# A four-layer decoder trunk: the second product of its MLPs by seven half-size products for eight

## The chip, the cores and the metric

The kernel runs on one NeuronCore of a Trainium2 chip. A core has a matrix engine (TensorE, PE in the profile, its weight loads PEld), three engines for elementwise work (VectorE, DVE; ScalarE, ACT; GpSimd, POOL) and SyncE (SP), which here only issues DMAs. The metric is the device time of one execution in microseconds (us); before the change it is 2807.53 us, the median of three runs (2807.37 to 2809.55).

## The reference

The program is a trunk of four pre-norm residual layers over 512 tokens and 1024 features in float32. Each layer has a token mixer (layers 0 and 3 dilated sliding-window attention, 1 attention over keys chosen by an indexer, 2 gated DeltaNet) and then the MLP, which is what the change touches:

```python
def squared_relu_mlp(h, w1, w2):            # h 512x1024, w1 1024x4096, w2 4096x1024
    return jnp.square(jax.nn.relu(h @ w1)) @ w2

for i in range(DEPTH):                      # DEPTH = 4
    ...
    x = x + y                               # y: the mixer of layer i
    x = x + squared_relu_mlp(rms_norm(x, norm_mlp[i]), mlp_w1[i], mlp_w2[i])
```

## The kernel before

Everything is kept transposed: a tile has 128 features on the partitions and the 512 tokens along the free axis. The residual stream `x` is eight such tiles. Products are made nearly exact in float32 out of the fast format fp32r by a split in a high and a low part: a factor is rounded to `hi`, `lo` is the factor less `hi`, and each product is three matmuls, hi by hi, hi by lo and lo by hi.

Weights come in chunks of 1 MB (1024 x 256, eight blocks of 128 rows). All chunks of the program have one running number n, and two buffers each for `raw`, `w_hi` and `w_lo`, taken in turn. A chunk goes through four engines: SP loads it (the load waits until POOL has split chunk n - 2), ACT rounds it to `w_hi` (`rounding`, L725, one instruction of 128x2048, after PE has finished chunk n - 2), POOL subtracts in four instructions of 128x512 (`split`, L578), and PE uses it for two output tiles.

An MLP is done in four quarters of 1024 hidden features; PE runs `mlp_quarter` (matmuls at L1877). Of a quarter's eight chunks the first four hold columns of w1: PE makes eight hidden tiles (tiles 0 to 7), alternately in PSUM banks 0 and 1, 24 matmuls of 512 columns each. Behind each, in `hidden`, DVE takes the tile out of PSUM with relu and the norm's factor (L1250), ACT squares it (L778) and rounds the square to `g_hi` (L780), and DVE subtracts to `g_lo` (L1253). The last four chunks hold w2: eight output tiles of 24 matmuls of 512 columns, each added to `x` by DVE (L1265). The first tile of the second half waits for `g_lo` block by block. Every engine runs its instructions in the order in which they are written: ACT has a rounding after every second hidden tile, and after every second output tile. In the last quarter of an MLP, DVE and ACT also prepare the next layer's norm behind each output tile (`prepare`, `low_x` L1228, `sum_square` L1222). Quarters 0 to 2 are a loop on ACT, DVE and POOL, quarters 1 to 3 on PE, and all four on SP.

## Time and profile before

| | |
|---|---|
| median of three runs | 2807.53 us |
| profiled execution, span | 2812.2 us |
| PE busy | 2726.8 us (97%) |
| DVE, ACT, POOL busy | 1037.2, 1082.5, 1387.4 us |
| MLP matmuls (L1877), of 512 columns | 6144, half of them of the second product |

The profiled execution has no time of its own but its span, which goes from the first to the last instruction of the program. A matmul's duration in the profile runs to its modelled end and overlaps the next one's: what a stream of matmuls costs is the distance from start to start. "Busy" of an engine is the union of its instructions.

### The profile page before, as it was taken

How to read it: one execution, taken by the hardware profiler on the slowest of the kernel's cores; microseconds unless marked ns; L12 is line 12 of the kernel's file. 1: busy time of each engine (PE TensorE's matmuls, PEld its weight loads, DVE VectorE, ACT ScalarE, POOL GpSimd, SP SyncE). 2: the span in 40 equal slices, each digit the busy share in tenths (PEclk: the TensorE clock that was granted, in tenths of full speed). 3: DMA queues.
4: the chain of work that ended last, by engine and by line, in shares of the span. 5: the costliest groups of instructions: out<-in, count | busy, mean ns of one | idle time of the engine just before them, and what ended most of it. 6: DMA issues, size and time to landing. Idle time of an engine off the chain costs nothing.

```text
span 2812.2 us, 37295 instructions
## 1 busy us (share of the span) xinstructions
PE 2726.8 (97%) x14594; PEld 2197.8 (78%) x14594; DVE 1037.2 (37%) x1936; ACT 1082.5 (38%) x1640; POOL 1387.4 (49%) x1074
## 2 busy tenths in 40 slices
PE   7999999999998999999899998999999999899999
PEld 5977678888765788888788887888888977688887
DVE  4035431113495522113777774311123044522112
ACT  4355442224346433224333444422234355533221
POOL 3566544454446354445535351544545576545443
PEclk9999999999999999999999999999999999999999
DMA  4331122323322123233311110223233322132232
GB/s 125 98 83 53 46 90 90 105 92 101 96 56 69 53 93 102 90 103 91 84 46 46 46 46 31 90 90 105 96 98 89 106 53 68 46 105 91 90 104 75
DMA packets 271884, 227.82 MB, mean 81 GB/s; under 512 B 29204, under 2 KB 259348, under 8 KB 271748
## 3 DMA queue, kind: packets, MB, share of 16 engines
q1 hardware_dynamic: 260880, 216.29, 25.4%
q10 hardware_dynamic: 10868, 9.66, 1.5%
...
## 4 chain that ended last, share of the span: by engine, by line
PE 91%; DVE 4%; ACT 2%; POOL 1%; issue 1%; DMA 0%; ACTq 0%; DVEq 0%; POOLq 0%
PE bank L1877 50%; PE bank L1786 20%; PE bank L1943 5%; PE bank L2170 2%; PE bank L2310 1%; PE bank L1918 1%; PE bank L1831 1%; PE bank L1996 1%; PE bank L2012 1%; POOL w_lo L578 1%; PE bank L1980 1%; PE bank L2097 1%; PE bank L2026 1%; PE bank L1973 1%; PE bank L2125 0%
## 5 line engine op out<-in xcount | busy, mean ns | idle before, releaser
L578 POOL TENSOR_TENSOR w_lo<-raw,w_hi 128x512 fp32r<-128x512 f32 x808 | 1080.9, 1367 | 1064.9 <-ACT w_hi L725 1064.9
L725 ACT ACTIVATE w_hi<-raw 128x2048 fp32r<-128x2048 f32 x202 | 385.5, 1908 | 456.9 <-PE bank L1877 423.3
L1877 PE MATMUL bank<-h_hi,w_hi 128*128 128x512 f32 x1024 | 400.8, 391 | 0.0
L1877 PE MATMUL bank<-h_hi,w_lo 128*128 128x512 f32 x1024 | 398.4, 389 | 0.0
L1877 PE MATMUL bank<-h_lo,w_hi 128*128 128x512 f32 x1024 | 398.4, 389 | 0.0
L1877 PE MATMUL bank<-g_hi,w_hi 128*128 128x512 f32 x1024 | 398.3, 389 | 0.0
L1877 PE MATMUL bank<-g_lo,w_hi 128*128 128x512 f32 x1024 | 398.3, 389 | 0.0
L1877 PE MATMUL bank<-g_hi,w_lo 128*128 128x512 f32 x1024 | 398.3, 389 | 0.0
L1786 PE MATMUL bank<-h_hi,w_hi 128*128 128x512 f32 x776 | 317.3, 409 | 10.1 <-POOL w_lo L578 7.2
L1786 PE MATMUL bank<-h_lo,w_hi 128*128 128x512 f32 x776 | 310.7, 400 | 0.0
L1786 PE MATMUL bank<-h_hi,w_lo 128*128 128x512 f32 x776 | 308.1, 397 | 0.0
L778 ACT ACTIVATE arena<-arena 128x512 f32<-128x512 f32 x128 | 80.9, 632 | 425.8 <-DVE arena L1250 425.8
L1250 DVE SCALAR_TENSOR_TENSOR arena<-bank,rs 128x512 f32<-128x512 f32 x128 | 88.5, 691 | 372.8 <-PE bank L1877 349.3
L1265 DVE TENSOR_TENSOR x<-x,bank 128x512 f32<-128x512 f32 x96 | 66.0, 687 | 431.6 <-PE bank L1877 431.6
L1877 PEld LDWEIGHTS bank<-h_lo,w_hi 128*128 128x128 f32 x1024 | 192.3, 188 | 41.3 <-issue 1.4
L1877 PEld LDWEIGHTS bank<-h_hi,w_hi 128*128 128x128 f32 x1024 | 192.3, 188 | 41.2 <-issue 1.4
L1877 PEld LDWEIGHTS bank<-g_hi,w_hi 128*128 128x128 f32 x1024 | 192.3, 188 | 39.9
L1877 PEld LDWEIGHTS bank<-g_lo,w_hi 128*128 128x128 f32 x1024 | 192.3, 188 | 39.9
L1877 PEld LDWEIGHTS bank<-g_hi,w_lo 128*128 128x128 f32 x1024 | 192.3, 188 | 39.8
L1877 PEld LDWEIGHTS bank<-h_hi,w_lo 128*128 128x128 f32 x1024 | 192.3, 188 | 39.7
L1786 PEld LDWEIGHTS bank<-h_hi,w_hi 128*128 128x128 f32 x776 | 147.8, 190 | 47.6 <-issue 9.6
L1786 PEld LDWEIGHTS bank<-h_lo,w_hi 128*128 128x128 f32 x776 | 147.6, 190 | 35.1 <-issue 6.7
...
## 6 DMA issues: line engine op xcount, KB each, us to landing
raw<-in_mlp_w SPq DMA_DIRECT2D x128, 1024.0 KB, 5.2
...
raw<-in_a_w_in SPq DMA_DIRECT2D x12, 1024.0 KB, 5.2
...
raw<-in_a_w_out SPq DMA_DIRECT2D x4, 1024.0 KB, 4.8
raw<-in_b_w_in SPq DMA_DIRECT2D x4, 1024.0 KB, 5.4
...
```

The costliest lines, as they stand in the source:

```text
L578: ins = nc.gpsimd.tensor_tensor(w_lo[s][:, k, :], raw[s][:, k, :], w_hi[s][:, k, :].bitcast(F32), ALU.subtract)
L725: nc.scalar.activation(w_hi[s][:], raw[s][:], ACT.Copy).then_inc(w_hi_done, 1)
L778: nc.scalar.activation(gsq[j % 2], relu_t[j % 2], ACT.Square).then_inc(gsq_done, 1)
L1250: nc.vector.scalar_tensor_tensor(relu_t[j % 2], lin_bank[j % 2][:], 0.0, rs, ALU.max, ALU.mult).then_inc(relu_done, 1)
L1265: nc.vector.tensor_tensor(x[:, c, :], x[:, c, :], lin_bank[c % 2][:], ALU.add).then_inc(x_added, 1)
L1786: mm = nc.tensor.matmul(o, lhsT, rhs, start=start, stop=stop)
L1831: mm = nc.tensor.matmul(lin_bank[t % 2][:], w[(n0 + f // 2) % 2][:].rearrange("p k n -> p (k n)")[:, c:c + P], a[:, f, :], start=k == 0, s ...
L1877: mm = nc.tensor.matmul(lin_bank[j][:], w[s][:, c, P * j:P * j + P], a[:, c, :], start=c + z == 0, stop=c == CT - 1 and z == 2)
L1918: nc.tensor.matmul(stat_bank[:], halves, sqs[Q % len(sqs)], start=True, stop=True).then_inc(ssq_done, 1)
L1943: mm = nc.tensor.matmul(bank[2 + b][:], keys, quads[w][:, c, :], start=half + c + z == 0, stop=half == 1 and c == 3 and z == 2)
L1973: mm = nc.tensor.matmul(bank[2 + half][:, 0:n], aq[f % 2][0][r, P * z:P * z + P], aq[f % 2][1][r, k0:k0 + n], start=True, stop=True)
L2170: mm = nc.tensor.matmul(out[z:z + HD], lhsT[:, z:z + HD], rhs, start=start, stop=stop)
```

## The change

Only the second product changes. The four chunks of w2 in a quarter (n + 4 to n + 7, here "halved" chunks; each makes two output tiles, and is numbered d = 0 to 3) are used by a Strassen scheme (its form with seven products and shared sums): the eight hidden tiles are taken in pairs p = 0 to 3 of an even and an odd tile, the chunk's two output tiles are the two halves of the outputs, and the tokens are halved (256 and 256). Seven products, each of 4 pairs x 3 matmuls of 256 columns, replace eight. They need four sums of weight blocks for each chunk (`w_sum`, then split in `ws_hi` and `ws_lo`) and three sums of hidden pieces for each pair (`pieces` 5 to 7, then `gt_hi` and `gt_lo`).

PE runs per chunk d the products A, B, C, B again, A again, D, A again, in PSUM half-banks; the later ones of a letter add to what stands there. DVE adds partial results to `x` after each in eight additions of 256 columns (`add_part`), and PE waits for some of them: the second B for the first two additions (`part_added`), the last A for the fifth (`x_added`).

DVE makes all weight sums (`summed_weights`, three instructions, of 1024, 512 and 512 columns) and half of their low parts (`low_sums`, 1024 columns), and the hidden sums (four of 256 columns a pair) and their low part (768 columns). ACT rounds the weight sums in a second instruction of 128x2048 in the same place as the chunk's own rounding. POOL has five instructions for a halved chunk in place of four. The first product, the mixers and the loads stay as they are, but for the values of semaphores; relu tiles lie in `sq` and the loops over quarters are written out on all engines.

```diff
+    def halved(n):
+        return CHUNKS[n][0] == "mlp" and CHUNKS[n][2] % 8 >= 4
...
+        w_sum = [part(4 * TOK).rearrange("p (k q n) -> p k q n", k=4, q=4) for _ in range(2)]
+        pieces = part(8 * HALF).rearrange("p (k n) -> p k n", k=8)
+        relu_t = sq
...
+        def quads(m):
+            return m.rearrange("p (q z) (n c) -> p (z n) q c", z=2, n=2)
+        def half_banks(d):
+            return [bank[k][:, 0:HALF] for k in ((2, 3, 4, 5), (6, 7, 0, 1))[d % 2]]
...
+            def split_halved(n):
+                s, v = n % 2, hi_value[n]
+                whole, high, low = (quads(m[s][:]) for m in (raw, w_hi, w_lo))
+                def of_weights(k):
+                    return nc.gpsimd.tensor_tensor(low[:, k], whole[:, k], high[:, k].bitcast(F32), ALU.subtract)
+                def of_sums(k):
+                    return nc.gpsimd.tensor_tensor(ws_lo[s][:, k], w_sum[s][:, k], ws_hi[s][:, k].bitcast(F32), ALU.subtract)
+                pool.wait_ge(w_hi_done, v - 1)
+                of_weights(0).then_inc(w_lo_done, 1)
+                pool.wait_ge(w_hi_done, v)
+                of_sums(1).then_inc(w_lo_done, 1)
+                of_weights(2).then_inc(w_lo_done, 1)
+                of_sums(3).then_inc(w_lo_done, 1)
+                of_weights(3).then_inc(w_lo_done, 1)
...
-            def rounding(n, raw_v=None, lin_v=None):
+            def rounding(n):
                 s = n % 2
-                raw_v = raw_value[n] if raw_v is None else raw_v
-                lin_v = tile0[max(n - 1, 0)] if lin_v is None else lin_v
-                act.wait_ge(raw_loaded[s], raw_v)
-                if not isinstance(lin_v, int) or lin_v > 0:
-                    act.wait_ge(lin_done, lin_v)
+                act.wait_ge(raw_loaded[s], raw_value[n])
+                if n >= 2:
+                    act.wait_ge(lin_done, tile0[n - 1])
                 nc.scalar.activation(w_hi[s][:], raw[s][:], ACT.Copy).then_inc(w_hi_done, 1)
+                if halved(n):
+                    act.wait_ge(ws_added, 3 * s_value[n])
+                    nc.scalar.activation(ws_hi[s][:], w_sum[s], ACT.Copy).then_inc(w_hi_done, 1)
...
+            def squares(Q, p, z):
+                g = 8 * Q + 2 * p + z
+                act.wait_ge(relu_done, g + 1)
+                if g >= 2:
+                    act.wait_ge(gt_done, 4 * (4 * Q + p) - 2) if z == 0 else act.wait_ge(gl_done, 3 * (4 * Q + p) - 1)
+                dst = pieces[:, 3:5, :] if z else pieces[:, 0:2, :][:, ::-1, :]
+                src = relu_t[z].rearrange("p (k n) -> p k n", k=2)
+                nc.scalar.activation(dst, src, ACT.Square).then_inc(gsq_done, 1)
+            def even_high(Q, p):
+                act.wait_ge(gt_done, 4 * (4 * Q + p) + 1)
+                nc.scalar.activation(by_half(g_hi[:, 2 * p, :]), pieces[:, 1:3, :], ACT.Copy).then_inc(gh_done, 1)
+            def odd_high(Q, p):
+                act.wait_ge(gsq_done, 8 * Q + 2 * p + 2)
+                nc.scalar.activation(by_half(g_hi[:, 2 * p + 1, :]), pieces[:, 3:5, :], ACT.Copy).then_inc(gh_done, 1)
+                act.wait_ge(gt_done, 4 * (4 * Q + p) + 4)
+                nc.scalar.activation(gt_hi[:, p], pieces[:, 5:8, :], ACT.Copy).then_inc(gh_done, 1)
             def mlp(li, i, m):
...
+                for q in range(QUARTERS):
+                    n, _, Q, X = quarter(li, q)
+                    for p in range(4):
+                        squares(Q, p, 0)
+                        even_high(Q, p)
+                        if p < 3:
+                            round_ahead(n + p)
+                        squares(Q, p, 1)
+                        odd_high(Q, p)
+                    round_ahead(n + 3)
+                    if q < QUARTERS - 1:
+                        for k in range(4, 8):
+                            round_ahead(n + k)
+                    else:
+                        residual(n + 4, X, m)
...
+            def summed_weights(n):
+                s, v = n % 2, 3 * (s_value[n] - 1)
+                whole = quads(raw[s][:])
+                dve.wait_ge(raw_loaded[s], raw_value[n])
+                if n >= 2 and halved(n - 2):
+                    dve.wait_ge(w_lo_done, lo_value[n - 2])
+                nc.vector.tensor_tensor(w_sum[s][:, 0:2], whole[:, 0::3], whole[:, 1:2].to_broadcast([P, 2, 4, P]),
+                                        ALU.add).then_inc(ws_added, 1)
+                dve.wait_ge(ws_added, v + 1)
+                nc.vector.tensor_tensor(w_sum[s][:, 2], w_sum[s][:, 1], whole[:, 0], ALU.add).then_inc(ws_added, 1)
+                dve.wait_ge(ws_added, v + 2)
+                nc.vector.tensor_tensor(w_sum[s][:, 3], w_sum[s][:, 2], whole[:, 2], ALU.add).then_inc(ws_added, 1)
+            def low_sums(n):
+                s = n % 2
+                dve.wait_ge(w_hi_done, hi_value[n])
+                nc.vector.tensor_tensor(ws_lo[s][:, 0::2], w_sum[s][:, 0::2], ws_hi[s][:, 0::2].bitcast(F32),
+                                        ALU.subtract).then_inc(ws_low, 1)
+            def relu(Q, T, p, z):
+                g = 8 * Q + 2 * p + z
+                dve.wait_ge(lin_done, T + 2 * p + z + 1)
+                if g >= 2:
+                    dve.wait_ge(gsq_done, g - 1)
+                nc.vector.scalar_tensor_tensor(relu_t[z], lin_bank[z][:], 0.0, rs, ALU.max, ALU.mult).then_inc(relu_done, 1)
+            def low(dst, src, high, value):
+                dve.wait_ge(gh_done, value)
+                nc.vector.tensor_tensor(dst, src, high.bitcast(F32), ALU.subtract).then_inc(gl_done, 1)
+            def even_tile(Q, T, p):
+                g, u = 8 * Q + 2 * p, 4 * Q + p
+                relu(Q, T, p, 0)
+                dve.wait_ge(gsq_done, g + 1)
+                nc.vector.tensor_tensor(pieces[:, 2, :], pieces[:, 1, :], pieces[:, 0, :], ALU.subtract).then_inc(gt_done, 1)
+                low(by_half(g_lo[:, 2 * p, :]), pieces[:, 1:3, :], by_half(g_hi[:, 2 * p, :]), 3 * u + 1)
+            def odd_tile(Q, T, p):
+                g, u = 8 * Q + 2 * p, 4 * Q + p
+                relu(Q, T, p, 1)
+                dve.wait_ge(gsq_done, g + 2)
+                nc.vector.tensor_tensor(pieces[:, 5, :], pieces[:, 4, :], pieces[:, 0, :], ALU.subtract).then_inc(gt_done, 1)
+                nc.vector.scalar_tensor_tensor(pieces[:, 6, :], pieces[:, 4, :], -1.0, pieces[:, 2, :], ALU.mult,
+                                               ALU.subtract).then_inc(gt_done, 1)
+                dve.wait_ge(gt_done, 4 * u + 3)
+                nc.vector.scalar_tensor_tensor(pieces[:, 7, :], pieces[:, 6, :], -1.0, pieces[:, 3, :], ALU.mult,
+                                               ALU.subtract).then_inc(gt_done, 1)
+                low(by_half(g_lo[:, 2 * p + 1, :]), pieces[:, 3:5, :], by_half(g_hi[:, 2 * p + 1, :]), 3 * u + 2)
+            def odd_sums(Q, p):
+                low(gt_lo[:, p], pieces[:, 5:8, :], gt_hi[:, p], 3 * (4 * Q + p) + 3)
...
+            def add_part(d, c, half, k, op, signal):
+                dst = x[:, c, HALF * half:HALF * half + HALF]
+                nc.vector.tensor_tensor(dst, dst, half_banks(d)[k], op).then_inc(signal, 1)
+            def first_parts(Q, d):
+                u = 4 * Q + d
+                dve.wait_ge(part_done, 6 * u + 1)
+                add_part(d, 2 * d, 0, 0, ALU.add, part_added)
+                dve.wait_ge(part_done, 6 * u + 2)
+                add_part(d, 2 * d + 1, 1, 1, ALU.subtract, part_added)
+            def down(li, Q, n, X, d, m):
+                u = 4 * Q + d
+                if d:
+                    first_parts(Q, d)
+                if m is not None and d:
+                    low_x(m, 2 * d - 1)
+                    sum_square(m, 2 * d - 1)
+                dve.wait_ge(part_done, 6 * u + 3)
+                dve.wait_ge(part_added, 6 * u + 1)
+                add_part(d, 2 * d, 0, 2, ALU.add, part_added)
+                dve.wait_ge(part_done, 6 * u + 4)
+                add_part(d, 2 * d, 1, 1, ALU.add, part_added)
+                dve.wait_ge(part_done, 6 * u + 5)
+                dve.wait_ge(part_added, 6 * u + 4)
+                add_part(d, 2 * d, 1, 0, ALU.add, x_added)
+                if d < 3:
+                    low_sums(n + d + 1)
+                dve.wait_ge(part_done, 6 * u + 6)
+                add_part(d, 2 * d + 1, 0, 3, ALU.subtract, part_added)
+                if m is not None:
+                    low_x(m, 2 * d)
+                    sum_square(m, 2 * d)
+                if d < 2:
+                    summed_weights(n + d + 2)
+                dve.wait_ge(lin_done, tile0[n + d] + 2)
+                dve.wait_ge(part_added, 6 * u + 5)
+                add_part(d, 2 * d + 1, 0, 0, ALU.subtract, part_added)
+                add_part(d, 2 * d + 1, 1, 0, ALU.subtract, x_added)
...
+                for q in range(QUARTERS):
+                    n, T, Q, X = quarter(li, q)
+                    for p in range(4):
+                        even_tile(Q, T, p)
+                        if p == 3:
+                            low_sums(n + 4)
+                        odd_tile(Q, T, p)
+                        if p == 3:
+                            first_parts(Q, 0)
+                        odd_sums(Q, p)
+                        if p in (1, 2):
+                            summed_weights(n + p + 3)
+                    last = q == QUARTERS - 1
+                    for d in range(4):
+                        down(li, Q, n + 4, X, d, m if last else None)
+                    if last and m is not None:
+                        dve.wait_ge(x_added, X + 8)
+                        low_x(m, CT - 1)
+                        sum_square(m, CT - 1)
...
+            def half_product(out, w, g, start, ready):
+                for p in range(4):
+                    if ready is not None:
+                        pe.wait_ge(gl_done, ready + 3 * p)
+                    high, low_ = w(p)
+                    a_hi, a_lo = g(p)
+                    for z, (l, a) in enumerate(((high, a_hi), (high, a_lo), (low_, a_hi))):
+                        mm = nc.tensor.matmul(out, l, a, start=start and p + z == 0, stop=p == 3 and z == 2,
+                                              skip_group_check=True)
+                return mm
+            def down(li, q, d):
+                n, _, Q, X = quarter(li, q)
+                n, u = n + 4 + d, 4 * Q + d
+                s, v = n % 2, lo_value[n] - 5
+                A, B, C, D = half_banks(d)
+                def weight(k):
+                    return lambda p: tuple(quads(m[s][:])[:, k, p, :] for m in (w_hi, w_lo))
+                def weight_sum(k):
+                    return lambda p: (ws_hi[s][:, k, p, :], ws_lo[s][:, k, p, :])
+                def hidden(z, half):
+                    return lambda p: tuple(m[:, 2 * p + z, HALF * half:HALF * half + HALF] for m in (g_hi, g_lo))
+                def hidden_sum(k):
+                    return lambda p: (gt_hi[:, p, k, :], gt_lo[:, p, k, :])
+                g = [12 * Q + k if d == 0 else None for k in (1, 2, 3)]
+                if d >= 2:
+                    pe.wait_ge(x_added, X + 2 * d - 2)
+                pe.wait_ge(w_lo_done, v + 1)
+                half_product(A, weight(0), hidden(0, 0), True, g[0]).then_inc(part_done, 1)
+                pe.wait_ge(w_lo_done, v + 2)
+                half_product(B, weight_sum(1), hidden(0, 1), True, None).then_inc(part_done, 1)
+                pe.wait_ge(w_lo_done, v + 3)
+                half_product(C, weight(2), hidden(1, 0), True, g[1]).then_inc(part_done, 1)
+                pe.wait_ge(w_lo_done, v + 4)
+                pe.wait_ge(part_added, 6 * u + 2)
+                half_product(B, weight_sum(3), hidden(1, 1), False, None).then_inc(part_done, 1)
+                pe.wait_ge(ws_low, s_value[n])
+                half_product(A, weight_sum(2), hidden_sum(1), False, g[2]).then_inc(part_done, 1)
+                pe.wait_ge(w_lo_done, v + 5)
+                half_product(D, weight(3), hidden_sum(2), True, None).then_inc(part_done, 1)
+                pe.wait_ge(x_added, X + 2 * d + 1)
+                half_product(A, weight_sum(0), hidden_sum(0), False, None).then_inc(lin_done, 2)
```

## Rows read from the trace of the kernel before

**Rows 1.** the page, busy time of each engine, share of the span, instructions

```profile
PE 2726.8 (97%) x14594; PEld 2197.8 (78%) x14594; DVE 1037.2 (37%) x1936; ACT 1082.5 (38%) x1640; POOL 1387.4 (49%) x1074
```

**Rows 2.** the page, the chain that ended last, share of the span by line

```profile
PE bank L1877 50%; PE bank L1786 20%; PE bank L1943 5%; PE bank L2170 2%; PE bank L2310 1%; PE bank L1918 1%; PE bank L1831 1%; PE bank L1996 1%; PE bank L2012 1%; POOL w_lo L578 1%; PE bank L1980 1%; PE bank L2097 1%; PE bank L2026 1%; PE bank L1973 1%; PE bank L2125 0%
```

**Rows 3.** the chain in order of time: start, us, what, count

```profile
367.81 342.77 PE bank L1877 x1512
...
1783.99 342.73 PE bank L1877 x1512
```

**Rows 4.** windows of two MLP quarters, busy time of each engine, granted clock

```profile
core 0: us, PE busy (x) PEld busy (x) DVE busy (x) ACT busy (x) POOL busy (x), PEclk, DMA share, GB/s
367.81:455.00 87.19, 87.19 (x386) 72.16 (x386) 16.84 (x25) 26.35 (x26) 40.98 (x32) 1.00 0.30 97
455.00:542.20 87.20, 87.20 (x386) 72.25 (x385) 16.93 (x25) 25.02 (x24) 41.82 (x33) 1.00 0.30 97
```

**Rows 5.** the page, a group of MLP matmuls, one of six alike

```profile
L1877 PE MATMUL bank<-g_hi,w_hi 128*128 128x512 f32 x1024 | 398.3, 389 | 0.0
```

**Rows 6.** timeline of PE, matmuls of 256 columns in mixer B: start, us

```profile
747.59 0.28 PE L1786 MATMUL bank<-w_hi,h_lo 128*128 128x256 f32 x1
...
748.78 0.28 PE L1786 MATMUL bank<-w_lo,h_hi 128*128 128x256 f32 x1
```

**Rows 7.** groups by line and shape on DVE, ACT and POOL

```profile
L1253 DVE TENSOR_TENSOR g_lo<-arena,g_hi 128x512 fp32r<-128x512 f32 x128 | 91.9, 718 | 174.3 <-ACT g_hi L780 174.3
L1250 DVE SCALAR_TENSOR_TENSOR arena<-bank,rs 128x512 f32<-128x512 f32 x128 | 88.5, 691 | 372.8 <-PE bank L1877 349.3 <-ACT rs L760 23.5
L1265 DVE TENSOR_TENSOR x<-x,bank 128x512 f32<-128x512 f32 x96 | 66.0, 687 | 431.6 <-PE bank L1877 431.6
...
L1694 DVE TENSOR_TENSOR arena<-arena,bank 128x256 f32<-128x256 f32 x48 | 19.8, 413 | 17.3 <-PE bank L2170 17.3
...
L725 ACT ACTIVATE w_hi<-raw 128x2048 fp32r<-128x2048 f32 x202 | 385.5, 1908 | 456.9 <-PE bank L1877 423.3 <-PE bank L1943 33.1 <-issue 0.5
L778 ACT ACTIVATE arena<-arena 128x512 f32<-128x512 f32 x128 | 80.9, 632 | 425.8 <-DVE arena L1250 425.8
...
L578 POOL TENSOR_TENSOR w_lo<-raw,w_hi 128x512 fp32r<-128x512 f32 x808 | 1080.9, 1367 | 1064.9 <-ACT w_hi L725 1064.9
```

**Rows 8.** timeline of DVE and of POOL in an MLP's quarters

```profile
690.12 0.68 DVE L1222 TENSOR_TENSOR ss<-ss,sq 128x512 f32<-128x512 f32 x1
...
694.90 0.89 DVE L1228 SCALAR_TENSOR_TENSOR h_lo<-x,par,h_hi 128x512 fp32r<-128x512 f32 x1
695.71 1.78 DVE L1222 TENSOR_TENSOR ss<-ss,sq 128x512 f32<-128x512 f32 x1
...
700.34 0.75 DVE L1228 SCALAR_TENSOR_TENSOR h_lo<-x,par,h_hi 128x512 fp32r<-128x512 f32 x1
...
692.70 5.94 POOL L578 TENSOR_TENSOR w_lo<-raw,w_hi 128x512 fp32r<-128x512 f32 x4 [4.95 <-ACT w_hi L725]
...
418.85 5.03 POOL L578 TENSOR_TENSOR w_lo<-raw,w_hi 128x512 fp32r<-128x512 f32 x4 [3.93 <-ACT w_hi L725]
```

**Rows 9.** timeline of all engines where a hidden tile ends

```profile
459.95 0.39 PE L1877 MATMUL bank<-h_hi,w_lo 128*128 128x512 f32 x1
...
460.17 0.39 PE L1877 MATMUL bank<-h_hi,w_hi 128*128 128x512 f32 x1
...
460.37 0.69 DVE L1250 SCALAR_TENSOR_TENSOR arena<-bank,rs 128x512 f32<-128x512 f32 x1 [2.70 <-PE bank L1877]
```

**Rows 10.** the page, DMA issues: KB each, median us to landing

```profile
raw<-in_mlp_w SPq DMA_DIRECT2D x128, 1024.0 KB, 5.2
```

**Rows 11.** timeline of PE after a wait, and the window around it

```profile
1336.83 0.67 PE L1786 MATMUL bank<-h_hi,w_hi 128*128 128x512 f32 x1 [2.60 <-POOL w_lo L578]
1337.29 0.63 PE L1786 MATMUL bank<-h_lo,w_hi 128*128 128x512 f32 x1
...
1336.00:1340.00 4.00, 3.17 (x8) 2.51 (x9) 0.38 (x1) 2.12 (x2) 2.64 (x3) 0.62 0.83 213
```

More of the change, by code:

```diff
@@ L31 @@
 CW = 256
+HALF = TOK // 2
 EPS = 1e-6
@@ L112, in trunk @@
         raw_value.append(at[n % 2])
+    def halved(n):
+        return CHUNKS[n][0] == "mlp" and CHUNKS[n][2] % 8 >= 4
+    hi_value, lo_value, s_value = [], [], []
+    for n in range(N):
+        hi_value.append((hi_value[-1] if n else 0) + (2 if halved(n) else 1))
+        lo_value.append((lo_value[-1] if n else 0) + (5 if halved(n) else 1))
+        s_value.append((s_value[-1] if n else 0) + halved(n))
     def added(li, mlp):
@@ L144, in trunk @@
         arena = sb("arena", [P, ARENA])
+        arena_at = nc.sbuf_base - 4 * ARENA
         taken = [0]
@@ L157, in trunk @@
         fresh()
-        relu_t = [part(TOK) for _ in range(2)]
-        gsq = [part(TOK) for _ in range(2)]
         x_tok = part(NB * DM).rearrange("p (b n) -> p b n", b=NB)
@@ L164, in trunk, with over_arena @@
         bmask_sb = part(RW)
+        fresh()
+        w_sum = [part(4 * TOK).rearrange("p (k q n) -> p k q n", k=4, q=4) for _ in range(2)]
+        pieces = part(8 * HALF).rearrange("p (k n) -> p k n", k=8)
+        relu_t = sq
+        over = [arena_at + 4 * taken[0]]
+        def over_arena(name, shape):
+            t = nc.alloc_sbuf_tensor_at(name, shape, F32R, offset=over[0])
+            over[0] += 4 * math.prod(shape[1:])
+            assert over[0] <= arena_at + 4 * ARENA, over[0]
+            return t
+        ws_hi = [over_arena(f"ws_hi{s}", [P, 4, 4, P]) for s in range(2)]
+        ws_lo = [over_arena(f"ws_lo{s}", [P, 4, 4, P]) for s in range(2)]
+        gt_hi, gt_lo = over_arena("gt_hi", [P, 4, 3, HALF]), over_arena("gt_lo", [P, 4, 3, HALF])
         bank = [ctx.enter_context(nc.psum_tensor(f"bank{k}", [P, TOK], F32)) for k in range(8)]
@@ L559, in _ @@
                     chunk(k)
-                with sp.Fori(0, QUARTERS) as q:
-                    mlp_chunks(i, n_mlp, q)
+                for k in range(8 * QUARTERS):
+                    mlp_chunk(n_mlp + k, i, k // 8, k % 8)
             for b in range(NB):
@@ L1266, in mlp @@
-                q = QUARTERS - 1
-                g = {k: G + 8 * q + k for k in range(9)}
-                hidden({k: T + 16 * q + k for k in range(9)}, g)
-                residual(T + 16 * q + 8, X + 8 * q, m)
+                for q in range(QUARTERS):
[17 more added lines that the diff above has]
+                        sum_square(m, CT - 1)
@@ L1854, in out_proj, with up @@
                         product(n0 + k, tile0[n0 + k] + j, (g_hi, g_lo), kt, lo, 24, yl_done, y_first[i], None)
-            def mlp_quarter(n, v_h, v_lo, v_x, v_relu, v_g, beside=None):
-                for k in range(8):
+            def up(li, q, beside):
+                n, T, Q, X = quarter(li, q)
+                for k in range(4):
                     s = (n + k) % 2
@@ L1879, in mlp_quarter @@
                         mm.then_inc(lin_done, 1)
-                        if t == 0 and beside is not None:
+                        if t == 0 and q == 0:
                             beside()
+            def half_product(out, w, g, start, ready):
[8 more added lines that the diff above has]
+                return mm
```

136 lines of the change are left out of this document (40 added, 96 removed).

## The prediction

> **What bounds the kernel now.** I read the page's busy times first: PE 97% of the span, the other engines half of it or less [rows 1]. Then the chain that ended last: 50% of it on the MLP matmuls, L1877 [rows 2]. Then that chain in order of time: three stretches of 1512 matmuls without any wait (the first and the last shown, 342.77 us), so 0.2267 us from start to start, and 24 of them, one tile, 5.44 us [rows 3]. So an MLP quarter is 16 tiles or 87.1 us, in which the windows show POOL busy 42 us, ACT 25 and DVE 17 [rows 4]. Here only PE counts; every other engine is hidden, and the reader should ask how far each is from not being so.
>
> **PE's own work.** The second product has half of the 6144 MLP matmuls, 3072 [rows 5]; by 0.2267 us that is 696.4 us. The change makes 4 layers x 4 quarters x 4 chunks x 7 products x 12 = 5376 of 256 columns. The trace has such matmuls in mixer B, with a new weight block for each: ten starts in 1.19 us, so 0.119 us [rows 6]. That is more than half of 0.2267. 5376 x 0.119 = 639.7 us: 56.7 us less, 3.5 a quarter. Bounds: half of 0.2267 gives 609 us (-87); 0.14, half the duration of 0.28 of such a record, gives 753 (+56), which the steady stretches speak against. I take 0.119.
>
> **What the other engines get.** Durations [rows 7]: DVE 0.69 us for 512 columns, 0.414 for 256, so by that slope 0.96 for 768 and 1.23 for 1024; ACT 0.63 for 512 and 1.91 for 2048, so 0.85 for 768; POOL 1.26 an instruction, the four of a split 5.03 alone [rows 8].
> DVE per quarter: eight relus 5.5; even tiles 4 x (0.42 + 0.69) = 4.4; odd tiles 4 x (3 x 0.42 + 0.69 + 0.96) = 11.6; four weight sums of 1.23 + 0.69 + 0.69 = 10.4; four low sums 4.9; 32 additions of 0.42 = 13.4. Together 50 us of 83.6, where it had 17. ACT gets 4 x 1.91 + 4 x 0.85 more, 36 in all. POOL gets four instructions more, 45 to 47 us. No engine passes PE by its sum, so the sums alone say that the change gains. The order says otherwise, through two things.
>
> **First, DVE and POOL share a way to SBUF.** In the last quarter of an MLP, DVE's `sum_square` (both inputs in SBUF) takes 0.68 us with POOL idle and 1.78 in a split; `low_x` 0.75 against 0.89; and the split with both of them in it takes 5.94 in place of 5.03 [rows 8]. So DVE waits for POOL's current instruction to end, does its own, then POOL does its next: in a split each DVE instruction with two SBUF inputs waits up to 1.1 us, and each costs POOL about 0.46. DVE's relus and additions have an input in PSUM and run at 0.69 in the split too [rows 7]. Before, one such instruction per tile (L1253) could meet a split. After, of DVE's 50 us 31 are of this kind; with POOL's 45 that is 76 us of the 83.6 of a quarter.
> The Trainium skill, page "SBUF — State Buffer", section "SBUF: two separate sides", has the pair of ports as a lock held for the whole instruction, taken by whoever starts first. The rows agree on who waits, but not on the whole length: POOL lost 0.46 per DVE instruction, not 0.69. By the whole length the quarter below comes out at 103 us and the run at 3070; that is rival D.
>
> **Second, the queues.** All times from the start of a quarter, a tile 5.44; a tile's end reaches DVE 0.2 after the next tile's first matmul [rows 9].
> *Even tile on DVE:* relu 0.69, ACT's square 0.67 with its hop, subtraction 0.42, ACT's rounding 0.71, low part 0.69: 3.2 us.
> *Odd tile:* relu 0.69, but ACT now has the chunk's rounding (1.91) ahead of the square. The rounding ends just as the square is due to begin, and it also starts POOL's split. DVE's hidden sums (0.42 x 3), low part (0.69) and low sums (0.96) then run against the split's four or five instructions: the first waits 0.5, three wait 1.0 each, 3.4 together. With 1.3 for the rest of the rounding and 0.65 for the square: 9 us.
> *Pairs p = 1 and 2* end with `summed_weights`, 2.7 us, and stand before the next relu on DVE.
> So a pair takes 12.2 us, and 14.1 with weight sums (some waits are then less), against 10.9 on PE. For p = 2 the chunk is the first halved one: ACT has a second 1.91 us before the square, and the pair takes 16.0.
> Placed one after the other: relu 0 starts at 5.6, relu 2 at 20.0 (it waited 2.2 for tile 1), relu 4 at 34.2, relu 6 at 50.2. PE's tile 6 needs relu 4 (bank 0): due at 32.6, begins at 34.9, **2.3 us late**. Its first product of the second half needs the low part of tile 6: PE is there at 46.9, DVE at 50.2 + 3.2 = 53.5, **6.6 late**. Product C needs tile 7's low part: after `low_sums` 1.23, relu, square, three sums and low part, 58.1; PE has done three, twelve and nine matmuls since 53.5, **1.8 late**. The second B needs two additions after that, **0.5 late**.
> In d = 0, DVE has after A's fifth addition (62.5): low sums 1.23, an addition 0.42, the next chunk's weight sums 2.7, with 3.2 of waiting for POOL's split, and two last additions, then the two first of d = 1: 71.8. PE could do the second B at 69.0: **2.8 late**. In d = 1 the same, less crowded, **1.4**. In d = 2 and 3 there are no weight sums: nothing.
> Sum 15.4 us of stalls a quarter against 3.5 saved: +11.9, so 99 us for 87.1. Bounds: none of it (-3.5), if DVE's pair stays under 10.9; and 16.3 (103 us) if the lock holds the full length. Two DVE instructions without a wait between them start 0.08 apart from end to start (694.90 + 0.89 is 695.79, the next has begun at 695.71 [rows 8]); about 45 such places could give back up to 3.6 a quarter. I take half, 1.8: +10.1 a quarter, +162 in all.
>
> **The last quarters.** In layers 0 to 2, `low_x` (0.75) and `sum_square` (0.69) for two tiles fall in each d, 2.9 us on a DVE that is late there in d = 0 and 1, more with POOL. That adds 2.9 to 11.6 a quarter; I take 6.6, +20 us. The start of the next mixer stays hidden: its first tile needs the last block only after seven of eight, 4.8 us in, and x's last addition comes 0.4 later than now.
>
> **Edits at nothing.** *POOL's splits and loads:* a halved chunk is split 1.26 later, its load goes out then and lands 5.2 us later [rows 10], while its use is a slot away; if that cover were gone, up to 1.3 a chunk, 16 x 4 x 1.3 = 83 at the very most. SP only waits for another value. *Written-out loops:* the first quarters were written out on PE before and are inside the dense stretches of [rows 3]. *Waits of PE:* the 16 tiles a quarter have one each now, at no visible cost.
>
> **Sum.** 2807.5 + 162 + 20 + 10 (the clock, rival C) = 3000 us. The profile's span, 2812.2, is 0.17% over the median; the sum is of differences and is put on the median.
>
> **The rivals.**
> *A, DVE and POOL do not hinder each other there.* For it: `low_x` at 0.89 shows that a lucky moment costs little, and L1253 has a mean of 0.718 though some of them meet a split [rows 7]. Against it: 1.78, and the new DVE chain is too long to fall between two of POOL's instructions. Then the pairs take 3.4 less, relu 4 is in time, the stalls are 2.0 + 1.8 + 0.5 = 4.3, less 3.5: +0.8 a quarter, 2820 us. Chance 0.12.
> *B, the other side: DVE's pair keeps under 10.9 us,* so that no wait of PE ends late at the turn from the first to the second product; that is the place, and the price of the turn is 0. It decides from there on. Then only the 56.7 us of PE count: 2751. For it: all engines have room by their sums. Against: 12 to 16 us for a pair by rows. Chance 0.06.
> *C, the clock.* After a wait of 2.6 us (POOL's w_lo, at 1336.8) PE starts its matmuls 0.46 us apart in place of 0.23; the granted clock of those 4 us is 0.62, so for most of them 1.2 GHz and not 2.4 [rows 11]. The stalls of 6.6 and 2.8 us are like that wait. If 3.5 us then run at half, each costs at most 1.7; behind the 6.6 the waits for C and B take it up, behind the 2.8 the next 1.4 does for the most part. So the forecast has 0.6 a quarter for it, +10 us. The rival is a clock that stays down from the turn through the whole chunk d = 0: 84 x 0.119 = 10.0 less the 2.3 of those waits, of which DVE's lateness in d = 1 hides about half: +4 a quarter, 3064 us. Chance 0.12.
> *D, the full-length lock* as told above: 2807.5 + 16 x (16.3 - 1.8) + 20 + 10 = 3070. Chance 0.10.
>
> **How the numbers follow.** Forecast 0.60, with 2940 to 3060 as its own range (the overlap taken in full or not at all, 2970 to 3028, and 30 us for the last quarters and the clock). The range 2885 to 3080 leaves out A and B. This kernel's three runs lie within 0.1%; I take 0.2% as what can be told. B is faster; of A's 0.12 a part lies within 0.2%, since its 13 us are near to that: faster 0.07, same 0.03, slower 0.90.
>
> **What would show it.** A quarter of some 97 us in place of 87, in the windows. 256-column matmuls at 0.119 in any stretch without a wait. PE waiting for DVE at the turn (`g_lo` of tile 6, the largest), for `x` additions in d = 0 and 1, and for relu 4; nearly none in d = 3. DVE's 256-column hidden sums at a median near 1.4 us, not 0.42. A trace with those at 0.42 gives A; no wait of PE at the turn gives B; a granted clock well under 1 behind the turn gives C. I would be wrong in kind if PE waited mostly for POOL's weights or for ACT.

## The result, and the profile after

The changed kernel takes 3003.56 us (median of four runs, 3001.3 to 3012.1), the kernel before 2808.54 in the same session: ratio 1.0696, 95% interval 1.0680 to 1.0712. It is 195 us slower; forecast were 3000.

The page after, against [rows 1, 2]: busy time of each engine, and the chain that ended last by engine.

```profile
PE 2748.8 (91%) x16898; PEld 2321.7 (77%) x16898; DVE 1788.4 (59%) x2896; ACT 1250.8 (42%) x1768; POOL 1541.0 (51%) x1138
...
PE 61%; DVE 23%; ACT 8%; issue 6%; POOL 2%; DMA 0%; ACTq 0%; DVEq 0%; POOLq 0%
```

PE has fallen from 97% to 91% of a longer span. DVE is busy for 751 us more and stands on a quarter of the chain, though its own share is only 59%.

The windows of layer 1's four MLP quarters, against [rows 4], columns as there; the quarters go from one quarter's first matmul to the next one's. Cut in the same way, layer 1's quarters of the kernel before are 87.92, 87.04, 87.04 and 87.04 us.

```profile
1027.12:1125.69 98.57, 88.53 (x532) 79.80 (x530) 65.64 (x89) 38.45 (x37) 50.90 (x36) 0.95 0.28 88
1125.69:1223.51 97.82, 86.94 (x531) 78.52 (x529) 64.36 (x84) 35.59 (x32) 52.17 (x36) 0.97 0.27 87
1223.51:1321.03 97.52, 88.84 (x530) 79.99 (x529) 63.08 (x84) 35.61 (x32) 51.06 (x36) 0.95 0.28 87
1321.03:1425.60 104.57, 90.58 (x529) 82.08 (x528) 74.78 (x96) 43.74 (x46) 51.10 (x35) 0.92 0.26 78
```

Quarters of 97.5 to 98.6 us for 87.0 to 87.9, and a last one of 104.6 for 87.0, where the next norm's work is on DVE too. DVE is busy 63 to 66 us where its instructions alone need 50 by the forecast's sum (47 in e1 below): the rest is waiting inside instructions. What PE waits for (in us over the run, times, longest):

```profile
PE bank L2046 <- DVE g_lo L1336: 82.6, 16, 5.9
PE bank L2046 <- DVE x L1366: 53.3, 23, 3.4
PE bank L2032 <- DVE sq L1332: 31.8, 16, 2.2
PE bank L1943 <- POOL w_lo L638: 13.1, 5, 4.6
```

L2046 is the second product, L2032 the first. The first three are the turn, the additions and the relu of tile 4, 168 us together, all DVE. L1943 is the mixers. DVE's groups by shape (from 356 us on), beside [rows 7]:

```profile
L1336 DVE TENSOR_TENSOR g_lo<-arena,g_hi 128x512 fp32r<-128x512 f32 x128 | 140.7, 1099 | 44.7 <-ACT g_hi L843 44.7
L1352 DVE SCALAR_TENSOR_TENSOR arena<-arena 128x256 f32<-128x256 f32 x64 | 79.1, 1236 | 0.0
L1355 DVE SCALAR_TENSOR_TENSOR arena<-arena 128x256 f32<-128x256 f32 x64 | 73.9, 1154 | 2.2
L1351 DVE TENSOR_TENSOR arena<-arena 128x256 f32<-128x256 f32 x64 | 59.7, 933 | 102.7 <-ACT arena L838 102.7
L1366 DVE TENSOR_TENSOR x<-x,bank 128x256 f32<-128x256 f32 x510 | 198.5, 415 | 223.3 <-PE bank L2046 223.1
```

The three hidden sums are of 256 columns, as the additions L1366 are; they take 0.93 to 1.24 us on the mean, the additions 0.415. The forecast's reason is that the sums read both inputs from SBUF while POOL splits; e1 tests it. How this looks in order of time, in the third pair of quarter 1125.69 (start, us; DVE, then ACT, then POOL):

```profile
1162.76 0.68 DVE L1332 SCALAR_TENSOR_TENSOR sq<-bank,rs 128x512 f32<-128x512 f32 x1
1166.27 1.11 DVE L1351 TENSOR_TENSOR arena<-arena 128x256 f32<-128x256 f32 x1 [2.83 <-ACT arena L838]
1167.30 1.51 DVE L1352 SCALAR_TENSOR_TENSOR arena<-arena 128x256 f32<-128x256 f32 x1
1168.84 1.40 DVE L1355 SCALAR_TENSOR_TENSOR arena<-arena 128x256 f32<-128x256 f32 x1
1170.16 1.78 DVE L1336 TENSOR_TENSOR g_lo<-arena,g_hi 128x512 fp32r<-128x512 f32 x1
...
1162.02 1.90 ACT L779 ACTIVATE w_hi<-raw 128x2048 fp32r<-128x2048 f32 x1
1163.83 1.90 ACT L782 ACTIVATE ws_hi<-arena 128x2048 fp32r<-128x2048 f32 x1
1165.63 0.61 ACT L838 ACTIVATE arena<-sq 128x512 f32<-128x512 f32 x1
...
1165.80 1.30 POOL L619 TENSOR_TENSOR ws_lo<-arena,ws_hi 128x512 fp32r<-128x512 f32 x1 [0.51 <-ACT ws_hi L782]
1167.05 1.48 POOL L616 TENSOR_TENSOR w_lo<-raw,w_hi 128x512 fp32r<-128x512 f32 x1
1168.49 1.47 POOL L619 TENSOR_TENSOR ws_lo<-arena,ws_hi 128x512 fp32r<-128x512 f32 x1
```

The relu is done at 1163.44, and its square on ACT begins at 1165.63, behind two roundings of weights. Then four instructions of DVE alternate with POOL's, one each per 1.44 us. PE's wait at the turn, and the window behind it:

```profile
1178.57 0.58 PE L2046 MATMUL bank<-g_hi,w_hi 128*128 128x256 f32 x1 [5.87 <-DVE g_lo L1336]
1178.95 0.41 PE L2046 MATMUL bank<-g_lo,w_hi 128*128 128x256 f32 x1
1179.16 0.41 PE L2046 MATMUL bank<-g_hi,w_lo 128*128 128x256 f32 x1
...
1178.60:1182.00 3.40, 3.40 (x16) 3.40 (x17) 2.67 (x5) 1.26 (x2) 0.00 (x0) 0.50 0.00 0
```

The granted clock behind the wait is 0.50, the lower level (1.2 GHz), and matmuls start 0.213 us apart, not 0.119.

### The profile page after: what moved, and what is told of

It reads as the page before. It is cut to its first block, busy times and chain, and to the rows that moved or that the text cites. A ratio compares the mean times of both kernels' runs of the same rounds, so it can differ in the third digit from the quotient of the medians.

```text
span 3010.3 us, 42130 instructions
## 1 busy us (share of the span) xinstructions
PE 2748.8 (91%) x16898; PEld 2321.7 (77%) x16898; DVE 1788.4 (59%) x2896; ACT 1250.8 (42%) x1768; POOL 1541.0 (51%) x1138
## 4 chain that ended last, share of the span: by engine, by line
PE 61%; DVE 23%; ACT 8%; issue 6%; POOL 2%; DMA 0%; ACTq 0%; DVEq 0%; POOLq 0%
PE bank L1943 19%; PE bank L2046 16%; PE bank L2032 6%; PE bank L2142 4%; DVE arena L1312 3%; DVE g_lo L1336 3%; ACT w_hi L779 2%; DVE arena L1352 2%; DVE arena L1355 2%; ACT arena L838 2%; DVE x L1366 2%; DVE arena L1315 2%; DVE arena L1351 2%; PE bank L2369 2%; DVE gt_lo L1336 1%
## 5 line engine op out<-in xcount | busy, mean ns | idle before, releaser
L638 POOL TENSOR_TENSOR w_lo<-raw,w_hi 128x512 fp32r<-128x512 f32 x552 | 748.5, 1384 | 638.4 <-ACT w_hi L779 638.4
L616 POOL TENSOR_TENSOR w_lo<-raw,w_hi 128x512 fp32r<-128x512 f32 x192 | 307.6, 1605 | 424.2 <-ACT w_hi L779 424.2
L2032 PE MATMUL bank<-h_hi,w_hi 128*128 128x512 f32 x1024 | 406.5, 397 | 31.8 <-DVE sq L1332 31.8
L2032 PE MATMUL bank<-h_hi,w_lo 128*128 128x512 f32 x1024 | 403.4, 394 | 0.0
L2032 PE MATMUL bank<-h_lo,w_hi 128*128 128x512 f32 x1024 | 403.0, 394 | 0.0
L1943 PE MATMUL bank<-h_hi,w_hi 128*128 128x512 f32 x776 | 318.9, 411 | 16.0 <-POOL w_lo L638 13.1
L1366 DVE TENSOR_TENSOR x<-x,bank 128x256 f32<-128x256 f32 x512 | 199.2, 415 | 224.3 <-PE bank L2046 224.1
L1943 PE MATMUL bank<-h_lo,w_hi 128*128 128x512 f32 x776 | 311.0, 401 | 0.0
L1943 PE MATMUL bank<-h_hi,w_lo 128*128 128x512 f32 x776 | 308.5, 398 | 0.0
L2032 PEld LDWEIGHTS bank<-h_hi,w_hi 128*128 128x128 f32 x1024 | 195.1, 191 | 79.5 <-issue 39.5
L2046 PE MATMUL bank<-g_hi,w_hi 128*128 128x256 f32 x512 | 153.1, 299 | 82.6 <-DVE g_lo L1336 82.6
L2032 PEld LDWEIGHTS bank<-h_lo,w_hi 128*128 128x128 f32 x1024 | 195.0, 190 | 41.5 <-issue 1.4
L2032 PEld LDWEIGHTS bank<-h_hi,w_lo 128*128 128x128 f32 x1024 | 194.7, 190 | 41.2
L619 POOL TENSOR_TENSOR ws_lo<-arena,ws_hi 128x512 fp32r<-128x512 f32 x128 | 186.5, 1457 | 49.9 <-ACT ws_hi L782 49.9
L2046 PE MATMUL bank<-g_hi,ws_hi 128*128 128x256 f32 x512 | 159.8, 312 | 53.7 <-DVE x L1366 53.3
L838 ACT ACTIVATE arena<-sq 128x512 f32<-128x512 f32 x128 | 80.1, 626 | 287.8 <-DVE sq L1332 287.8
L1943 PEld LDWEIGHTS bank<-h_hi,w_hi 128*128 128x128 f32 x776 | 148.1, 191 | 54.0 <-POOL w_lo L638 15.4
L1943 PEld LDWEIGHTS bank<-h_lo,w_hi 128*128 128x128 f32 x776 | 148.4, 191 | 35.1 <-issue 6.7
L1943 PEld LDWEIGHTS bank<-h_hi,w_lo 128*128 128x128 f32 x776 | 148.0, 191 | 33.3 <-issue 2.4
L2046 PEld LDWEIGHTS bank<-g_hi,w_hi 128*128 128x128 f32 x512 | 103.1, 201 | 86.6 <-DVE g_lo L1336 85.8
L1336 DVE TENSOR_TENSOR g_lo<-arena,g_hi 128x512 fp32r<-128x512 f32 x128 | 140.7, 1099 | 44.7 <-ACT g_hi L843 44.7
```

What stands on the lines that cost most here:

```text
L616: return nc.gpsimd.tensor_tensor(low[:, k], whole[:, k], high[:, k].bitcast(F32), ALU.subtract)
L619: return nc.gpsimd.tensor_tensor(ws_lo[s][:, k], w_sum[s][:, k], ws_hi[s][:, k].bitcast(F32), ALU.subtract)
L638: ins = nc.gpsimd.tensor_tensor(w_lo[s][:, k, :], raw[s][:, k, :], w_hi[s][:, k, :].bitcast(F32), ALU.subtract)
L838: nc.scalar.activation(dst, src, ACT.Square).then_inc(gsq_done, 1)
L1336: nc.vector.tensor_tensor(dst, src, high.bitcast(F32), ALU.subtract).then_inc(gl_done, 1)
L1366: nc.vector.tensor_tensor(dst, dst, half_banks(d)[k], op).then_inc(signal, 1)
```

## The experiments

Nine kernels; each ratio is to the kernel before in the same session. "Quarter" is a steady one, from first matmul to first matmul; "last" are the last quarters of layers 0 to 2. The first quarter of each MLP is left out: it is some 1 to 2.5 us longer in every kernel, the one before included.

| kernel | median us | ratio to before (95%) | quarter | last |
|---|---|---|---|---|
| before | 2808.5 | | 87.0 | 87.0 |
| changed | 3003.6 | 1.0696 (1.0680 to 1.0712) | 97.5 to 97.8, one 99.0 | 102.3 to 104.7 |
| e1 POOL only writes | 2808.1 | 0.9995 (0.9986 to 1.0005) | 86.7 | 87.5 |
| e2 the same, kernel before | 2808.2 | 1.0000 (0.9991 to 1.0010) | | |
| e3 no weight sums | 2883.0 | 1.0264 (1.0248 to 1.0279) | 90.1 | 93.8 to 95.1 |
| e4 extra matmuls at the turn | 3007.4 | 1.0707 (1.0693 to 1.0722) | 97.5 to 97.8 | 103.3 to 103.7 |
| e5 squares first on ACT | 2957.5 | 1.0523 (1.0507 to 1.0539) | 94.0 to 95.8 | 100.0 to 102.6 |
| e6 = e1 and e3 | 2774.5 | 0.9873 (0.9858 to 0.9888) | 84.6 | 84.6 |
| e7 orders of DVE and ACT anew | 2807.1 | 0.9992 (0.9983 to 1.0001) | 85.5 | 91.5 to 92.1 |
| e8 the last quarters' order too | 2811.6 | 1.0005 (0.9996 to 1.0014) | 85.5 | 93.3 to 94.4 |
| e9 the last quarters again | 2797.2 | 0.9956 (0.9942 to 0.9970) | 85.5 | 88.6 |

**e1: POOL's MLP splits write and don't read.**

```
-    return nc.gpsimd.tensor_tensor(low[:, k], whole[:, k], high[:, k]..., ALU.subtract)
+    return nc.gpsimd.memset(low[:, k]..., 0.0)
```

The same stands in `of_sums`, and in the split of the w1 chunks, where a first strip of 8 columns is still subtracted. The low parts of the weights are left out; all else stays.

> The changed kernel, but POOL makes the low parts of the MLP's weights (and half of those of the weight sums) by filling 512 columns with zeros, which reads nothing from SBUF, in place of a subtraction of two SBUF inputs; so the low parts of the weights are left out, and all else, waits and order too, stays. Theory (DVE and POOL hinder each other, on top of the order of the queues): DVE's hidden sums come down to 0.42 us each, an MLP quarter from 97.8 to about 87, the run to about 2815 us. Rival, the order of the queues alone: the quarter stays at 97 to 98 and the run at 3000. Rival, each half of it: 2900.

Measured: 2808.1. DVE's groups:

```profile
L1342 DVE TENSOR_TENSOR g_lo<-arena,g_hi 128x512 fp32r<-128x512 f32 x128 | 88.2, 689 | 44.7 <-ACT g_hi L849 44.7
L1357 DVE TENSOR_TENSOR arena<-arena 128x256 f32<-128x256 f32 x64 | 27.2, 426 | 122.7 <-ACT arena L844 122.7
L1358 DVE SCALAR_TENSOR_TENSOR arena<-arena 128x256 f32<-128x256 f32 x64 | 26.8, 419 | 0.0
L1361 DVE SCALAR_TENSOR_TENSOR arena<-arena 128x256 f32<-128x256 f32 x64 | 27.2, 425 | 2.2
...
L616 POOL MEMSET w_lo<- 128x512 f32 x192 | 101.3, 528 | 523.5 <-ACT w_hi L785 523.5
```

Every DVE instruction is back at its own length (g_lo 0.689 for 1.099, the sums at 0.42), with the queue order unchanged, and the 195 us are gone: at the turn PE waits 1.4 us and, for C, 1.3, where it waited 4.4 to 6.0. But POOL's instructions are also shorter, 0.53 us for 1.26, so DVE might only meet them less often. The timeline answers that, where the two run at the same time (quarter 1150.99; DVE, then POOL):

```profile
1188.97 0.43 DVE L1361 SCALAR_TENSOR_TENSOR arena<-arena 128x256 f32<-128x256 f32 x1
1189.31 0.68 DVE L1342 TENSOR_TENSOR g_lo<-arena,g_hi 128x512 fp32r<-128x512 f32 x1
...
1188.62 0.52 POOL L619 MEMSET ws_lo<- 128x512 f32 x1
1189.09 0.53 POOL L616 MEMSET w_lo<- 128x512 f32 x1
```

Both DVE instructions have two inputs in SBUF and run while memsets run, and neither takes longer than alone. Nor do PE or DVE wait for `w_lo` in the MLPs of the changed kernel, so there POOL's own speed held nothing up.

**e2: the same edit in the kernel before**, the control.

> The same edit in the kernel before (zeros for the low parts of the MLP's weights, three of a chunk's 1024 by 256 left out but for a first strip of 8 columns). Control: every theory expects no change, 2807 us within 0.3%, since PE does not wait in its MLPs.

2808.2 us, no change: in the kernel before, the meeting of DVE and POOL costs no time.

**e3: the weight sums 8 columns wide**, plain blocks in their place; the splits stay.

```
-    nc.vector.tensor_tensor(w_sum[s][:, 2], w_sum[s][:, 1], whole[:, 0], ALU.add)
+    nc.vector.tensor_tensor(w_sum[s][:, 2, 0, 0:8], whole[:, 1, 0, 0:8], whole[:, 0, 0, 0:8], ALU.add)
```

This is one of the three instructions; rounding and low parts take the plain weights in instructions of the same size, so the sums are left out of the product.

> The changed kernel, but the weight sums are left out: DVE's three instructions for them (1024, 512 and 512 columns) have 8 columns each, and ACT, POOL and DVE take the weights themselves where they took the sums, in instructions of the same size. Theory (10.4 us of DVE work a quarter, 5.2 of it ahead of relu 4 and relu 6, is what makes DVE's pair longer than PE's): stalls at tile 6 and in d = 1 and 2 go, that at the turn shrinks from 6.0 to 2 to 3 us, a quarter takes about 89.5, the run 2850 to 2865 us. Rival, ACT's second rounding and the split of POOL set the pair: at most 2 us less a quarter, 2970. Rival, the turn is set by tile 7's chain alone: the stall at the turn stays, 2920.

2883.0: most of the loss goes (120 of 195), but the time is 18 us over the expected range. Tile 6 is in time, the turn still costs 3.9 us and d = 1 up to 0.6. I had the steady quarter at 89.5 (it is 90.1) and the last ones too short (93.8 to 95.1).

**e4: 40 extra matmuls while PE waits at the turn**, to keep it busy.

> The changed kernel, with 40 further matmuls of 256 columns into an unused bank on PE at the turn of each quarter, ahead of the first wait for g_lo of tile 6 (stall 4.4 to 6.0 us): 4.8 us of PE work inside the stall; nothing is left out. Granted clock behind the turn: 1.0. Theory (the half clock behind the turn is taken up by the waits for C and the second B, which follow DVE): these waits reappear with about 1.5 to 2 us, the quarter stays at 97.8 and the run within 0.3% of 3003 us. Rival, the half clock costs its full 2 us a quarter: 2970 us.

3007.4, no gain. The stall is filled (in 8 of the 16 quarters the extra matmuls even end 0.4 us after `g_lo` is there), and the granted clock behind the turn is 1.00 in all 16. What the half clock had covered is bare: C waits 1.0 to 1.3 us and the second B 0.29, together a little less than the 1.5 to 2 expected, and the second B of d = 1 waits 2.58 in every steady quarter. Behind this stall the clock costs nothing, since DVE is late there anyway.

**e5: on ACT, the odd tile's square and rounding ahead of the weights' rounding.**

```
                         even_high(Q, p)
-                        if p < 3:
-                            round_ahead(n + p)
                         squares(Q, p, 1)
                         odd_high(Q, p)
+                        if p < 3:
+                            round_ahead(n + p)
```

> ScalarE alone is reordered: the square of a pair's odd tile and its rounded squares stand ahead of the chunk's rounding of weights (1.9 us), which stood ahead of them. Nothing else moves, no work is left out. My theory (PE's stalls come from DVE's chain of a pair, which is lengthened by that rounding and by POOL's split): the chain loses about 1.3 us of the rounding, tile 6 is in time, the turn shrinks from 6.0 to some 3 us: a quarter of 94.6 for 97.8, 2950 us (2930 to 2970). Rival (the whole excess is the meeting of DVE with POOL, and the order on ScalarE only moves when they meet): POOL's split starts later too, so the same meetings come later and the time stays within 5 us of 3003. Second rival: the later split makes PE wait for POOL's w_lo, over 3020.

2957.5, in the range: 46 us for moving one call. The turn is 2.8 to 4.7 us for 4.4 to 6.0. Tile 6 was to be in time and is not: it is 0.9 to 1.9 late for 2.1, and in 12 of 16 quarters now waits for POOL's `w_lo`. So the second rival has a small part too, 28 waits on POOL:

```profile
PE bank L2046 <- DVE x L1366: 56.2, 23, 4.6
PE bank L2046 <- DVE g_lo L1336: 53.1, 18, 4.5
PE bank L2032 <- POOL w_lo L638: 14.1, 28, 0.9
```

**e6: e1 and e3 together.**

> Both taken away together: POOL's subtractions in the MLP are memsets (low parts of the weights are zero) and DVE's weight sums are 8 columns wide, with copies of plain blocks in the place of the sums. PE's instructions stay as they are. Theory (PE's 256-column matmuls do save 3.5 us a quarter, and what the change loses is all DVE's lateness): a quarter of 84.5 with 0.9 left at the turn, 2765 us (2755 to 2775), ratio 0.985. Rival (the first memset run broke even with the kernel before because the Strassen product saves nothing on PE, and its waits were hidden by something else): a quarter of 86.7 again, 2807.

2774.5, inside the expected range, at its upper edge; the quarter is 84.6, as expected (84.5). PE waits 1.0 us in it: 87.1 - 3.5 + 1.0. So the seven products of 256 columns do save 3.5 us a quarter on PE. e1 had spent the same saving on waits of 3.0.

**e7: all the work, another order** on DVE and ACT. The calls of a quarter stand in a table each, here their middle:

```
+DVE_ORDER = (... ("relu", 3), ("gtO", 1), ("relu", 4), ("ws", 0), ("gtE", 2), ("lowO", 1), ("relu", 5), ...
+    ("gtO", 3), ("lowO", 3), ("A1_", 0), ("B1_", 0), ("C_", 0), ("lowT", 3), ("ws", 1), ("B2_", 0), ...
+ACT_ORDER = (... ("hiE", 1), ("rd", 3), ("sq", 3), ("hiO", 1), ("hiT", 1), ("sq", 4), ("rd", 4), ("hiE", 2), ...
```

("ws" are the weight sums, "gt" the hidden sums, "low" low parts, "rd" the rounding of weights, A1 to C the additions.)

> All work kept, the instruction order on DVE and ScalarE written anew: squares of both tiles ahead of any rounding of weights, sums of squares and relus taken by need, the weight sums moved to where DVE has time (the first in the third pair, the others behind the first two parts of chunks d = 0 and d = 2), the two parts of C and B taken alternately. Theory (a queue's order costs the change its gain; DVE and POOL still hinder each other as before): by the same durations PE waits 2 us a quarter for 14: a quarter of 85.3 to 86.3 against 87.1 before, 2780 to 2800 us, ratio 0.990 to 0.997. Rival (the hindrance between DVE and POOL sets it, whatever the order): well over 2850.

2807.1: 196 us less than the changed kernel, no better than the one before, 7 us over the range. The windows of a steady and of a last quarter:

```profile
1065.15:1150.62 85.47, 84.89 (x528) 76.26 (x528) 58.95 (x85) 35.09 (x32) 53.08 (x36) 1.00 0.32 99
1236.08:1327.60 91.52, 85.97 (x528) 76.53 (x528) 70.33 (x97) 43.22 (x46) 53.41 (x36) 1.00 0.32 93
```

The steady one is what the theory gives (85.3 to 86.3), 1.6 under the kernel before. DVE is still busy 59 us, and the hidden sums take 0.67 to 0.96 on the mean: less than the 0.93 to 1.24 of the changed kernel, more than their own 0.42. So the new order also makes DVE and POOL meet less: of the 17 us a quarter between e1's 47.3 us of busy DVE and the changed kernel's 64.4, some 12 are left. The last quarters, which I had taken along as steady ones, are 4.4 to 5.1 over the kernel before and give the win back.

**e8: an order of their own for the last quarters.**

> All work kept. The steady quarters as in the run reordered before; in the last quarter of layers 0 to 2 the next norm's low parts and sums of squares no longer stand behind the second and the sixth addition of each chunk but where the additions leave room, and ScalarE takes its share of them in another order. There three quarters of 91.5 to 92.1 us lost what thirteen of 85.5 had won. Theory (that loss is again queue order on DVE): the three come to 87.0, 13 to 14 us in all: 2793 us (2790 to 2798), ratio 0.995. Rival (a DVE with 36 us of work in the 40 of that second product cannot keep up in any order): 2805 to 2810, no better than before. Second rival (the later low parts hold up the next mixer): the quarters shorten, the time does not.

2811.6, 14 us over the range and just above the first rival's: the last quarters take 93.3 to 94.4 us. DVE, POOL and PE at the end of one:

```profile
1322.25 1.17 DVE L1329 SCALAR_TENSOR_TENSOR h_lo<-x,par,h_hi 128x512 fp32r<-128x512 f32 x1
1323.34 1.78 DVE L1323 TENSOR_TENSOR ss<-ss,sq 128x512 f32<-128x512 f32 x1
1325.04 1.77 DVE L1329 SCALAR_TENSOR_TENSOR h_lo<-x,par,h_hi 128x512 fp32r<-128x512 f32 x1
1326.74 1.75 DVE L1323 TENSOR_TENSOR ss<-ss,sq 128x512 f32<-128x512 f32 x1
1328.41 0.93 DVE L1413 TENSOR_TENSOR x<-x,bank 128x256 f32<-128x256 f32 x2
...
1322.82 6.79 POOL L656 TENSOR_TENSOR w_lo<-raw,w_hi 128x512 fp32r<-128x512 f32 x4
...
1329.40 0.58 PE L2093 MATMUL bank<-gt_hi,ws_hi 128*128 128x256 f32 x1 [3.19 <-DVE x L1413]
```

I had planned this place as if POOL were idle. It splits the last weights of the MLP and the next mixer's first chunk there, and four instructions of 0.7 us take 1.2 to 1.8 each, ahead of an addition that PE waits for. It is the change's own failure once more, in small.

**e9: that work kept out of those places.**

```
-    2), ("X", 3), ("D_", 2), ("F_", 2), ("lows", 3), ("A1_", 3), ("B1_", 3), ("C_", 3), ("X", 4), ("X", 5),
-    ("B2_", 3), ("A2_", 3), ("D_", 3), ("X", 6), ("F_", 3))
+    2), ("X", 3), ("D_", 2), ("X", 4), ("F_", 2), ("lows", 3), ("A1_", 3), ("B1_", 3), ("C_", 3), ("X", 5),
+    ("B2_", 3), ("A2_", 3), ("D_", 3), ("F_", 3), ("X", 6))
```

("X" is one block's low part and sum of squares for the next norm.)

> As the run before, with the next norm's work of the last quarters placed anew: behind the first additions of chunk d = 1 and around the additions of d = 2 and 3, never with two of its low parts ahead of the second B's additions while POOL splits; all work kept. In the run before, these quarters were 93 to 94 us: PE waited 2.9 us in d = 1 and 3.4 in d = 3 for additions that stood behind two of the norm's pairs on DVE, which POOL's split of the next mixer's chunk drew out to 1.8 us an instruction. Theory (a queue order that leaves those places free keeps the steady quarters' win): 88 to 89.5 us for the 91.5 to 92.1 of the first reordered run, so 8 to 10 us less than its 2807: 2799 us (2795 to 2803), ratio 0.9965. Rival (DVE is full in these quarters, and any order pays about 5 us each): 2805 to 2812.

2797.2 (2794.5 to 2799.3), as expected, with last quarters of 88.6; the rival, that any order pays there, is out. PE's waits on DVE's additions in the second product, over the whole run, are down to:

```profile
PE bank L2093 <- DVE x L1413: 10.1, 22, 1.1
```

Ratio 0.9956, interval 0.9942 to 0.9970: the only kernel with all of its work that beats the one before, by 0.4%.

## Why the prediction was right

**PE's own work** held: dense 256-column matmuls start 0.119 us apart, and e6's quarter shows the 3.5 us.

**DVE against POOL** held in kind and size. The hidden sums were to have a median near 1.4 us; the three lines have medians of 1.10, 1.51 and 1.40 (0.42 in a quarter's last pair, where POOL does not split). That it is this meeting is shown by e1; e2 shows that the edit alone gains nothing. The Trainium skill, page "SBUF — State Buffer", section "SBUF: two separate sides", lets a DVE instruction with two SBUF inputs be held off only by a GpSimd one that reads SBUF; e1, where POOL's instructions only write, agrees. The lock for the whole length, rival D, failed: POOL's starts in the pair above are 1.44 us apart with a DVE instruction of 0.42 between, 1.25 without one (1165.80 to 1167.05), so POOL loses 0.19 and not 0.42, as it lost 0.46 and not 0.69 before.

**The queues**, step by step (quarter 1125.69; starts of the relus relative to it in the trace, forecast in brackets): relu 0 5.7 (5.6), relu 2 20.1 (20.0), relu 4 34.0 (34.2), relu 6 49.6 (50.2). Tile 6 late 2.1 (2.3). Turn 6.0 (6.6) in nine quarters; 4.4 in the seven whose clock fell behind tile 6's wait (granted 0.87 up to the turn for 1.00), since PE came later. C and the second B 1.8 + 0.5: hardly to be seen, since PE ran at half clock there, but back in e4 with 1.0 to 1.3 and 0.29. d = 1, second B: 1.9 to 2.8, and 2.58 in e4 (2.8). d = 2: 0 or 1.5 (1.4). d = 3: nothing (nothing). The steady quarter: 10.5 to 10.8 over before but for one of 11.9, forecast 10.1 and 0.6 for the clock.

**Mis-sized.** *The last quarters* were forecast 6.6 each over a steady one and are 4.5, 6.9 and 5.8: 17 us for 20. *The start of the next mixer* was to stay hidden, and that step failed. The four MLP stretches give 190 us of the 198 by which the spans differ, and 8 lie outside them: the stretches from one MLP to the next are 4.1, 2.2 and 5.3 us longer, the one ahead of the first MLP 3.2 shorter. The forecast looked at `x` alone. In all three places PE's first matmul waits 1.9 to 2.0 us for POOL's `w_lo`, which it did not before: ACT begins to round that chunk 5.4 us ahead of the MLP's end where it was 8.8, behind work that waits for DVE's additions, and POOL's split follows. In the first and the third the clock is low behind this wait and costs 1.8 us more. The last 2 us, and the 3.2 ahead of the first MLP, are not traced.

**The clock.** Rival C failed as forecast: the clock does not stay down through d = 0. In quarter 1125.69 that chunk, 10.0 us when dense, takes 18.6: 6.0 of wait and 2.6 of low clock. But the forecast's own term was too small. It had at most 1.7 us behind the turn, and read [rows 11] as starts 0.46 apart, which is the first step only; the next are 0.43. Over a whole steady quarter matmuls at the lower clock cost 2.8 to 4.8 us (6.1 in the one of 99.0), not 0.6. This does not show in the time, because the waits are shorter by as much: 9.1 to 11.5 us. Together they are 14.1 to 14.4 on a dense 83.4, and the forecast had 15.4 - 1.8 + 0.6 = 14.2. That these agree so closely is partly luck: the 1.8 was half of a bound, chosen without a row, and time that the forecast had as waits went to the low clock.

**Rival A** was what the kernel does if DVE and POOL do not meet: e1 ran it, 2808 where A said 2820: its waits are 1.4 + 1.3 + 0.3 us a quarter where A had 2.0 + 1.8 + 0.5. **Rival B** wanted no wait at the turn; e6, with work left out, comes nearest (2774.5), and B's 2751 would have needed no waits at all.

What the prediction did not ask is whether the loss belongs to the extra work or to the order it came in. It takes both the old order and the meeting with POOL to lose it: e1 keeps the order, takes the meeting away and is 195 us faster; e7 keeps all the work and most of the meeting, changes the order and is 196 us faster, e9 206.
